# The low parts of the weights: 11/16 of each half on VectorE, 5/16 on GpSimd

## The chip, the cores and the metric

The kernel runs on one core of one Trainium2 chip. The metric is the device time of one execution in microseconds, as the median of three runs; less is better. The engines are TensorE (PE), VectorE (DVE), ScalarE (ACT), GpSimd (POOL) and the DMA queue of SyncE (SP).

## The reference

Two transformer-like blocks in float32 on 256 tokens of width 1024, batch 1. What matters here is only that nearly all of it is products of a small activation with large weights that are each used once:

```python
def first_block(x, ...):
    h = _rmsnorm(x, g_mix_pre)
    proj = h @ w_in + b_in                 # 1024 x 3328: pool, q, k, v, two gates
    y_pool = _multiscale_pool(...); y_attn = _sliding_window_sink_attention(...)
    merged = g_pool * (y_pool @ w_branch_pool) + g_attn * (y_attn @ w_branch_attn)
    x = x + _rmsnorm(merged @ w_out, g_mix_post)
    h2 = _rmsnorm(x, g_mlp_pre)
    return x + _rmsnorm(square(relu(h2 @ w_up)) @ w_down, g_mlp_post)   # hidden width 4096

def second_block(x, c, ctx, ...):          # two layers, latent and context rows
    for i in range(2):
        modulation = silu(c) @ mod_w[i] + mod_b[i]      # 1024 x 6144, shift, scale and gate
        o = short_conv_mixer(...) if i == 0 else mla_mixer(...)
        h = h + g1 * o
        h = h + g2 * swiglu(modulate(rms_norm(h), sh2, sc2), w_gate, w_up, w_down)  # hidden width 2816
    return h_lat
```

## The kernel before

To reach float32 accuracy, each product is made of three matmuls on split operands: a value is written as `hi + lo`, where `hi` is the value rounded to the type that TensorE reads (fp32r) and `lo` is the rest; the products are hi x hi, lo x hi and hi x lo (lines 401 to 403, in `product`). The modulation vectors need two (lines 435 and 436, in `mod_product`).

The weights come as one stream of 107 chunks, in the order of their use. A chunk is 128 partitions by 4096 columns (2 MB; some are 3072, 2304, 2048 or 1024 columns wide). Everything about it is double-buffered in two slots: `raw` (as loaded), `w_hi` and `w_lo`. For each chunk:

- SyncE's queue loads it into `raw` (line 328) as soon as `w_lo` of the chunk two before, which used the same slot, is complete (`lo_ready`).
- ScalarE waits for the load and for the products that read this slot last, and writes `w_hi` in two halves (line 947), each of which raises `hi_ready`.
- VectorE subtracts, `w_lo = raw - w_hi`, in two halves (line 1430, in `split`), each of which raises `lo_ready`.
- TensorE waits for the first half's `lo_ready` in `chunk()` and for the second half's in `split_half(0)`, in the middle of the first product of the chunk, or where its first column of the second half is.

The halves are given by

```python
half = width // 2
return [(h * half, (h + 1) * half) for h in range(2)]
```

The engines run their programs strictly in order. Where a split stands between the other work of ScalarE and VectorE is written out by hand. VectorE has much other work: it takes products out of PSUM (`gated<-bank,gate`, line 1792; `h<-silu,bank`, line 1843), adds to the residual rows (`x<-x,gated`, line 1794), makes the low parts of the activations (`act_lo`, line 1455; `h_lo`, lines 1707, 1848 and 2058), applies the norms (`scaled`, lines 1468 and 1471; `post_norm`, lines 1529 and 1530). GpSimd has no program at all.

The stages in order of time: the first block's input projection, attention and branches to about 170 us; norms and modulation to 205; the MLP in 4 turns of 57 us to 434, each of six chunks, two of which are modulation chunks; norms to 475; the convolution mixer to 640; norms; the FFN of the first layer to 1030, its main part in 4 turns of 72 us with one modulation chunk each; latent attention with four groups of heads to 1290; the output projection and norm to 1335; the second FFN to the end.

Of the kernel before, what the change touches and what calls it, by code (L numbers as in the profile page):

```python
# [21 lines left out]
CHUNK = 4096  # L22
# [15 lines left out]
MH = 16  # L38
GH = 4
# [8 lines left out]
SECTIONS = (  # L48
    ("w_in", 2, 4096), ("w_kv", 1, 2048), ("w_gates", 4, 4096), ("w_branch", 4, 4096), ("w_out", 2, 4096), ("mod_scale", 2, 4096),
    ("mlp", 24, 4096), ("mod_gate0", 2, 4096), ("conv_in", 8, 3072), ("conv_out", 2, 4096),  # L50
    ("mod_gate1", 2, 4096), ("ffn0_first", 1, 4096), ("ffn0_half", 1, 2048), ("ffn0", 19, 4096),
    ("mod_gate2", 2, 4096), ("mla_in", 2, 4096), ("mod_gate3", 1, 4096), ("mla_q", 4, 2304), ("mla_kv", 4, 1024),
    ("mod_gate3_half", 1, 4096), ("mla_out", 2, 4096),
    ("ffn1", 16, 4096), ("ffn1_half", 1, 2048),
)
STREAM = sum(n for _, n, _ in SECTIONS)
# [60 lines left out]
def build(nc, a, out):  # L117
    f32, f32r = mybir.dt.float32, mybir.dt.float32r
    ACT, ALU, AX = mybir.ActivationFunctionType, mybir.AluOpType, mybir.AxisListType
# [4 lines left out]
    def at(name, shape, offset, dtype=f32):  # L124
        return nc.alloc_sbuf_tensor_at(name, shape, dtype, offset=base + offset)

    K = 1024
    raw = at("raw", [P, 2, CHUNK], 0)
    w_hi = at("w_hi", [P, 2, CHUNK], 32 * K, f32r)
    w_lo = at("w_lo", [P, 2, CHUNK], 64 * K, f32r)  # L130
# [99 lines left out]
    def table(name, n, parts=P, j=0):  # L230
        return tab[0:parts, TAB[name] + j:TAB[name] + j + n]
# [15 lines left out]
    S = nc.alloc_semaphore  # L247
    loaded = [S("loaded0"), S("loaded1")]
    hi_ready = S("hi_ready")
    lo_ready = S("lo_ready")  # L250
    const_loaded = S("const_loaded")
    x_loaded = [S("x_loaded0"), S("x_loaded1")]
    bias_loaded = S("bias_loaded")
# [53 lines left out]
    WQ, WKV = QKT * GH * QK, KVT * COLS  # L307

    def halves_of(width):


        half = width // 2
        return [(h * half, (h + 1) * half) for h in range(2)]

    with nc.Block() as block:


        @block.sync
        def _(sp):
            n = Count()  # L320

            def load(section, k, width):
                c = n.step("chunk")
                slot = (n.n["chunk"] - 1) % 2
                if n.n["chunk"] > 2:
                    sp.wait_ge(lo_ready, 2 * n.at("chunk", 2))
                src = a[section][k] if isinstance(k, int) else a[section][bass.ds(k, 1)].rearrange("o p n -> (o p) n")
                sp.dma_start(raw[:, slot, 0:width], src).then_inc(loaded[slot], 16)


            for t in range(NT):
                sp.dma_start(x[:, t, :], a["x"][t * P:(t + 1) * P, :]).then_inc(x_loaded[t], 16)
            sp.dma_start(tab[:, :], a["tab"]).then_inc(const_loaded, 16)
            sp.dma_start(cols[:, :], a["cols"]).then_inc(const_loaded, 16)
            sp.dma_start(rows[:, :], a["rows"].rearrange("(o n) -> o n", o=1).to_broadcast([P, NROW])).then_inc(const_loaded, 16)
            for section, chunks, width in SECTIONS:
                first = 0
                if section == "mla_kv":
                    continue
                if section == "mla_q":  # L340
                    with n.loop(sp, chunks, chunk=2) as i:
                        load("mla_q", i, WQ)
                        load("mla_kv", i, WKV)
                    continue
                while first < chunks and (chunks < 8 or n.n["chunk"] < 2):
                    load(section, first, width)
                    first += 1
                turns = (chunks - first) // 2
                if turns:
                    with n.loop(sp, turns, chunk=2) as i:  # L350
                        load(section, i * 2 + first, width)
                        load(section, i * 2 + first + 1, width)
                if (chunks - first) % 2:
                    load(section, chunks - 1, width)

            for t in range(NT):
                sp.wait_ge(x_ready, X_UPDATES - NT + 1 + t)
                sp.dma_start(out[t * P:(t + 1) * P, :], x[:, t, :]).then_inc(out_done, 16)
            sp.wait_ge(out_done, 16 * NT)


        @block.tensor
        def _(te):
            n = Count()

            def chunk():
                n.step("chunk")
                split_half(1)
                return (n.n["chunk"] - 1) % 2

            def split_half(back):

                te.wait_ge(lo_ready, 2 * n.at("chunk") - back)

            def weights(s, j0, j1):
                return w_hi[:, s, j0:j1], w_lo[:, s, j0:j1]
# [14 lines left out]
            def product(dst, terms, second=None, also=None, before_last=None):  # L391


                for j, ((sh, sl), (mh, ml)) in enumerate(terms):
                    if before_last and j == len(terms) - 1:
                        before_last()
                    if j == second:
                        split_half(0)
                        if also:
                            also()  # L400
                    te.matmul(dst, sh, mh, start=(j == 0), stop=False)  # L401
                    te.matmul(dst, sh, ml, start=False, stop=False)  # L402
                    last = te.matmul(dst, sl, mh, start=False, stop=(j == len(terms) - 1))  # L403
                return last
# [21 lines left out]
            def mod_product():  # L426
                s = chunk()
                m = n.step("mod")
                if n.n["mod"] > 1:
                    te.wait_ge(mod_row_ready, n.at("mod", 1))  # L430
                for k in range(KT):
                    if k == KT // 2:
                        split_half(0)
                    h, l = weights(s, k * COLS, (k + 1) * COLS)
                    te.matmul(mod_ps[:, :], cond_w[:, k, :], h, start=(k == 0), stop=False)  # L435
                    last = te.matmul(mod_ps[:, :], cond_w[:, k, :], l, start=False, stop=(k == KT - 1))  # L436
                last.then_inc(mod_done, 1)
# [30 lines left out]
            for k, width in enumerate((COLS, COLS, 256)):  # L468
                s = chunk()
# [184 lines left out]
            s = chunk()  # L654
# [45 lines left out]
            s = chunk()  # L700
            for tt in range(2 * NT):
                conv_out(s, tt, tt == 0)
            s = chunk()
# [55 lines left out]
            s = chunk()  # L759
# [7 lines left out]
            s = chunk()  # L767
# [7 lines left out]
            s = chunk()  # L775
            for tt in range(2 * NT):
# [3 lines left out]
                first = 0 if tt < NT else 256  # L780
# [147 lines left out]
        def _(act):  # L928
            n = Count()

            def split(width=CHUNK):
                n.step("split")
                c = n.n["split"]
                if c > STREAM:
                    return
                s = (c - 1) % 2
                turns = 16 * ((c + 1) // 2)
                if n.turn is not None:
                    turns = n.turn * (8 * n.per["split"]) + turns
                act.wait_ge(loaded[s], turns)  # L940
                if n.n["unit"]:
                    act.wait_ge(gemm_done, n.at("unit"))
                if n.n["mod"]:
                    act.wait_ge(mod_done, n.at("mod"))
                for first, end in halves_of(width):
                    part = slice(first, end)
                    act.activation(w_hi[:, s, part], raw[:, s, part], ACT.Copy).then_inc(hi_ready, 1)  # L947

# [72 lines left out]
            for k in range(3):  # L1021
                split()
                n.step("unit", 2)
# [390 lines left out]
        def _(ve):  # L1414
            n = Count()
# [6 lines left out]
            def split(width=CHUNK):  # L1422
                n.step("split")
                if n.n["split"] > STREAM:
                    return
                s = (n.n["split"] - 1) % 2
                for half, (first, end) in enumerate(halves_of(width)):
                    part = slice(first, end)
                    ve.wait_ge(hi_ready, 2 * n.at("split") - 1 + half)
                    ve.tensor_tensor(w_lo[:, s, part], raw[:, s, part], w_hi[:, s, part].bitcast(f32),  # L1430
                                     ALU.subtract).then_inc(lo_ready, 1)
# [126 lines left out]
            for t in range(NT):  # L1558
                heads = proj[:, t, Q0:V0].rearrange("p (h d) -> p h d", d=HD)
                lo, hi = heads[:, :, 0:8], heads[:, :, 8:16]  # L1560
                c = table("cos1", 8, j=8 * t).rearrange("p (o d) -> p o d", o=1).to_broadcast([P, 10, 8])
                s = table("sin1", 8, j=8 * t).rearrange("p (o d) -> p o d", o=1).to_broadcast([P, 10, 8])
# [650 lines left out]
```

## Time and profile before

| what | value |
|---|---|
| time, median of 3 runs | 1531.93 us (1528.47 to 1532.8) |
| the profiled execution: its time, its span | 1531.93 us, 1530.1 us |
| TensorE busy, matmuls | 1435.3 us, 94% of the span |
| VectorE busy | 923.9 us, 60% |
| of that, the subtractions for `w_lo` (214) | 460.3 us |
| ScalarE busy | 651.2 us, 43% |
| GpSimd busy | 0.2 us, 4 instructions |
| mean granted clock of TensorE | 0.969 of full speed |
| loaded from memory | 213.7 MB, 140 GB/s |

The profile is of one execution. Busy time is the time in which an engine executes an instruction; waits on semaphores are not in it. Matmuls overlap one another, so that one lasts longer than the distance to the next. In the rows below an arrow in brackets names what ended the idle time in front of an instruction.

### The profile page before, as it was taken

To read this page: it belongs to the slowest core of one execution; us is meant where nothing else is said; L and a number is where in the kernel's file an instruction comes from. 1 tells how busy PE (TensorE), PEld (TensorE's weight loads), DVE (VectorE), ACT (ScalarE), POOL (GpSimd) and SP (SyncE) were. 2 spreads that over 40 slices of the span, in tenths; PEclk is the share of its full clock that TensorE was granted. 3 is DMA by queue.
4 is the path that set the end of the run, shared out by engine and by line. 5 is a ranking of instruction groups with operands and counts; after the bars stand their busy time and mean duration, and the time that the engine had idled before them with its cause. 6 is when DMAs were issued, how large, how long until landed. Compare 5 with 4: busy or idle time off the path is not lost.

```text
span 1530.1 us, 18989 instructions
## 1 busy us (share of the span) xinstructions
PE 1435.3 (94%) x7536; PEld 1208.1 (79%) x7536; DVE 923.9 (60%) x1136; ACT 651.2 (43%) x743; POOL 0.2 (0%) x4
## 2 busy tenths in 40 slices
PE   6999889999989999999999999998989988899998
PEld 5877678888867887777888888886867766699997
DVE  5677676765666655766444453537566656646567
ACT  5364555544552222543132322225535554543442
POOL 0000000000000000000000000000000000000000
PEclk9999989999999999999999999999879998899999
DMA  8525565655642233233332414213221121344541
GB/s 307 196 94 219 196 234 217 229 208 222 245 154 83 83 143 118 75 118 127 148 120 99 163 56 164 96 69 121 93 76 46 69 96 61 120 166 171 203 175 56
DMA packets 18152, 215.58 MB, mean 141 GB/s; under 512 B 1960, under 2 KB 2984, under 8 KB 4784
## 3 DMA queue, kind: packets, MB, share of 16 engines
q1 hardware_dynamic: 16416, 209.67, 36.6%
q10 hardware_dynamic: 1680, 5.13, 0.9%
q8 instruction: 40, 0.66, 0.2%
q14 instruction: 16, 0.13, 0.0%
HBM read 213.74 MB, written 1.05 MB: 140 GB/s over the span
## 4 chain that ended last, share of the span: by engine, by line
PE 81%; DVE 10%; ACT 5%; issue 2%; ACTq 0%; DMA 0%; DVEq 0%
PE bank L401 24%; PE bank L403 23%; PE bank L402 23%; DVE w_lo L1430 6%; PE turned L418 3%; ACT w_hi L947 3%; PE small L831 2%; PE bank L825 2%; PE mod_ps L435 1%; PE mod_ps L436 1%; PE small L448 1%; PE small L458 1%; DVE x L1794 0%; DVE gated L1792 0%; DVE scaled L1471 0%
## 5 line engine op out<-in xcount | busy, mean ns | idle before, releaser
L1430 DVE TENSOR_TENSOR w_lo<-raw,w_hi 128x2048 fp32r<-128x2048 f32 (+1 forms) x214 | 460.3, 2193 | 82.5 <-ACT w_hi L947 82.1
L947 ACT ACTIVATE w_hi<-raw 128x2048 fp32r<-128x2048 f32 (+1 forms) x214 | 380.7, 1827 | 247.4 <-PE bank L403 179.9
L401 PE MATMUL bank<-act_hi,w_hi 128*128 128x256 f32 (+1 forms) x1208 | 400.1, 331 | 21.2 <-DVE w_lo L1430 12.8
L402 PE MATMUL bank<-act_lo,w_hi 128*128 128x256 f32 (+1 forms) x1208 | 396.7, 328 | 0.0
L403 PE MATMUL bank<-act_hi,w_lo 128*128 128x256 f32 (+1 forms) x1208 | 396.6, 328 | 0.0
L401 PEld LDWEIGHTS bank<-act_hi,w_hi 128*128 128x128 f32 x1208 | 232.4, 192 | 52.8 <-issue 17.8
L402 PEld LDWEIGHTS bank<-act_lo,w_hi 128*128 128x128 f32 x1208 | 232.5, 192 | 19.4
L403 PEld LDWEIGHTS bank<-act_hi,w_lo 128*128 128x128 f32 x1208 | 232.4, 192 | 19.2
L401 PE MATMUL bank<-w_hi,h_hi 128*128 128x512 f32 x392 | 157.3, 401 | 2.7 <-DVE h_lo L1848 1.5
L402 PE MATMUL bank<-w_lo,h_hi 128*128 128x512 f32 x392 | 155.9, 398 | 0.0
L403 PE MATMUL bank<-w_hi,h_lo 128*128 128x512 f32 x392 | 155.8, 397 | 0.0
L1843 DVE TENSOR_TENSOR h<-silu,bank 128x512 f32<-128x512 f32 x22 | 15.1, 687 | 133.7 <-PE bank L403 133.7
L401 PEld LDWEIGHTS bank<-w_hi,h_hi 128*128 128x128 f32 x392 | 74.4, 190 | 21.1 <-DVE h_lo L1848 2.5
L401 PE MATMUL bank<-w_hi,act_hi 128*128 128x512 f32 (+1 forms) x224 | 85.8, 383 | 4.9 <-DVE w_lo L1430 3.6
L403 PEld LDWEIGHTS bank<-w_hi,h_lo 128*128 128x128 f32 x392 | 74.3, 189 | 17.8
L435 PE MATMUL mod_ps<-w_hi,cond_w 128*128 128x512 f32 x192 | 79.9, 416 | 8.7 <-DVE w_lo L1430 5.1
L402 PEld LDWEIGHTS bank<-w_lo,h_hi 128*128 128x128 f32 x392 | 74.3, 189 | 16.8
L402 PE MATMUL bank<-w_lo,act_hi 128*128 128x512 f32 (+1 forms) x224 | 84.7, 378 | 0.0
L403 PE MATMUL bank<-w_hi,act_lo 128*128 128x512 f32 (+1 forms) x224 | 84.6, 378 | 0.0
L1792 DVE TENSOR_TENSOR gated<-bank,gate 128x512 f32<-128x512 f32 x84 | 57.7, 687 | 41.1 <-PE bank L403 40.8
L436 PE MATMUL mod_ps<-w_lo,cond_w 128*128 128x512 f32 x192 | 78.3, 408 | 0.0
L1246 ACT ACTIVATE h_hi<-h 128x512 fp32r<-128x512 f32 x22 | 13.8, 628 | 97.2 <-DVE h L1843 97.2
(235 smaller groups left out, 1604.0 us busy)
## 6 DMA issues: line engine op xcount, KB each, us to landing
raw<-in_ffn SPq DMA_DIRECT2D x35, 2048.0 KB, 7.6
raw<-in_mlp SPq DMA_DIRECT2D x24, 2048.0 KB, 8.4
raw<-in_mod_gate SPq DMA_DIRECT2D x7, 2048.0 KB, 8.2
raw<-in_conv_in SPq DMA_DIRECT2D x8, 1536.0 KB, 6.5
raw<-in_w_gates SPq DMA_DIRECT2D x4, 2048.0 KB, 8.4
raw<-in_w_branch SPq DMA_DIRECT2D x4, 2048.0 KB, 8.6
raw<-in_mla_q SPq DMA_DIRECT2D x4, 1152.0 KB, 5.1
raw<-in_w_in SPq DMA_DIRECT2D x2, 2048.0 KB, 13.1
```

The costliest lines, as they stand in the source:

```text
L401: te.matmul(dst, sh, mh, start=(j == 0), stop=False)
L402: te.matmul(dst, sh, ml, start=False, stop=False)
L403: last = te.matmul(dst, sl, mh, start=False, stop=(j == len(terms) - 1))
L418: last = te.transpose(dst[0:m, j * P:(j + 1) * P], src, ident)
L435: te.matmul(mod_ps[:, :], cond_w[:, k, :], h, start=(k == 0), stop=False)
L436: last = te.matmul(mod_ps[:, :], cond_w[:, k, :], l, start=False, stop=(k == KT - 1))
L448: last = te.matmul(small[:, 2 * j:2 * j + 2], mod_row[0:4, j * P:(j + 1) * P], table("sel_col", 2, 4), start=True, stop=True)
L825: te.matmul(bank[u % 2][:, :], qgT[:, h, t * P:(t + 1) * P], kgT[:, h, :], start=True, stop=True).then_inc(scores_done, 1)
L831: last = te.matmul(small[:, u * VD:(u + 1) * VD], prT[:, u % 2, j, :], vg[:, j, h, :], start=(j == 0), stop=(j == 3))
L947: act.activation(w_hi[:, s, part], raw[:, s, part], ACT.Copy).then_inc(hi_ready, 1)
L1430: ve.tensor_tensor(w_lo[:, s, part], raw[:, s, part], w_hi[:, s, part].bitcast(f32), ALU.subtract).then_inc(lo_ready, 1)
L1792: ve.tensor_tensor(gated[:, k, :], b[:, :], gate[:, g, cb * COLS:(cb + 1) * COLS], ALU.mult).then_inc(gemm_read, 1)
```

## The change

The subtraction of each half is divided between two engines. Of a half's columns VectorE keeps the first 11/16 and GpSimd, which gets a program of its own, takes the last 5/16. GpSimd waits for the same `hi_ready` values as VectorE and raises a semaphore of its own, `lo_ready_pool`; the load queue and TensorE wait for both. ScalarE's conversion still goes by whole halves. The number and the order of the other instructions stay as they are.

```diff
+    lo_ready_pool = S("lo_ready_pool")
...
-        return [(h * half, (h + 1) * half) for h in range(2)]
+        return [(h * half, h * half + half * 11 // 16, (h + 1) * half) for h in range(2)]
...
                     sp.wait_ge(lo_ready, 2 * n.at("chunk", 2))
+                    sp.wait_ge(lo_ready_pool, 2 * n.at("chunk", 2))
...
+        @block.gpsimd
+        def _(pool):
+            n = Count()
+
+            def split(width=CHUNK):
+                n.step("chunk")
+                s = (n.n["chunk"] - 1) % 2
+                for _, share, end in halves_of(width):
+                    part = slice(share, end)
+                    pool.wait_ge(hi_ready, n.step("half"))
+                    pool.tensor_tensor(w_lo[:, s, part], raw[:, s, part], w_hi[:, s, part].bitcast(f32),
+                                       ALU.subtract).then_inc(lo_ready_pool, 1)
+
+            def splits(chunks):
+                with n.loop(pool, chunks // 2, chunk=2, half=4):
+                    split()
+                    split()
+                if chunks % 2:
+                    split()
+
+            names = [name for name, _, _ in SECTIONS]
+            before = sum(c for _, c, _ in SECTIONS[:names.index("mla_q")])
+            groups = MH // GH
+            splits(before)
+            with n.loop(pool, groups, chunk=2, half=4):
+                split(WQ)
+                split(WKV)
+            splits(STREAM - before - 2 * groups)
...
                 te.wait_ge(lo_ready, 2 * n.at("chunk") - back)
+                te.wait_ge(lo_ready_pool, 2 * n.at("chunk") - back)
...
-                for first, end in halves_of(width):
+                for first, _, end in halves_of(width):
                     part = slice(first, end)
                     act.activation(w_hi[:, s, part], raw[:, s, part], ACT.Copy).then_inc(hi_ready, 1)
...
-                for half, (first, end) in enumerate(halves_of(width)):
-                    part = slice(first, end)
+                for half, (first, share, _) in enumerate(halves_of(width)):
+                    part = slice(first, share)
                     ve.wait_ge(hi_ready, 2 * n.at("split") - 1 + half)
                     ve.tensor_tensor(w_lo[:, s, part], raw[:, s, part], w_hi[:, s, part].bitcast(f32),
                                      ALU.subtract).then_inc(lo_ready, 1)
```

GpSimd's program goes by chunks of 4096 columns throughout except in the attention section; the widths of the narrower sections outside it (`w_kv`, `conv_in`, `ffn0_half`, `ffn1_half`) are taken as 4096 there, as they are in VectorE's and ScalarE's programs, which convert the whole slot.

## Rows read from the trace of the kernel before

**Rows 1.** The page: the span, busy time, and shares of the chain that ended last.

```profile
span 1530.1 us, 18989 instructions
...
PE 1435.3 (94%) x7536; PEld 1208.1 (79%) x7536; DVE 923.9 (60%) x1136; ACT 651.2 (43%) x743; POOL 0.2 (0%) x4
...
PE 81%; DVE 10%; ACT 5%; issue 2%; ACTq 0%; DMA 0%; DVEq 0%
PE bank L401 24%; PE bank L403 23%; PE bank L402 23%; DVE w_lo L1430 6%; PE turned L418 3%; ACT w_hi L947 3%; PE small L831 2%; PE bank L825 2%; PE mod_ps L435 1%; PE mod_ps L436 1%; PE small L448 1%; PE small L458 1%; DVE x L1794 0%; DVE gated L1792 0%; DVE scaled L1471 0%
```

**Rows 2.** Groups by line and form on VectorE: busy us, mean ns | idle before.

```profile
L1430 DVE TENSOR_TENSOR w_lo<-raw,w_hi 128x2048 fp32r<-128x2048 f32 x198 | 444.6, 2288 | 81.8 <-ACT w_hi L947 81.5 <-DVE z_pad L1756 0.3
...
L1471 DVE TENSOR_SCALAR scaled<-turned,coef,mod_col 128x128 f32<-128x128 f32 x112 | 37.1, 403 | 12.0 <-PE turned L418 11.8
...
L1430 DVE TENSOR_TENSOR w_lo<-raw,w_hi 128x1152 fp32r<-128x1152 f32 x8 | 10.5, 1355 | 0.6 <-ACT w_hi L947 0.6
```

**Rows 3.** The chain that ended last, in an MLP turn: start us, us, what.

```profile
274.53 1.93 ACT w_hi L947
```

**Rows 4.** Who waited for whom on TensorE: us in total, times, longest us.

```profile
PE bank L401 <- DVE w_lo L1430: 18.5, 18, 3.6
PE mod_ps L435 <- DVE w_lo L1430: 5.1, 2, 3.2
```

**Rows 5.** Timeline of TensorE, waits for `w_lo`: start us, us, what [idle before].

```profile
18.59 0.80 PE L401 MATMUL bank<-w_hi,act_hi 128*128 128x512 f32 x1 [3.61 <-DVE w_lo L1430]
...
194.00 0.80 PE L435 MATMUL mod_ps<-w_hi,cond_w 128*128 128x512 f32 x1 [3.20 <-DVE w_lo L1430]
...
202.19 0.39 PE L401 MATMUL bank<-act_hi,w_hi 128*128 128x256 f32 x1 [1.48 <-DVE w_lo L1430]
...
204.39 0.38 PE L401 MATMUL bank<-act_hi,w_hi 128*128 128x256 f32 x1 [0.51 <-DVE w_lo L1430]
...
278.90 0.38 PE L401 MATMUL bank<-act_hi,w_hi 128*128 128x256 f32 x1 [0.69 <-DVE w_lo L1430]
...
281.03 0.39 PE L401 MATMUL bank<-act_hi,w_hi 128*128 128x256 f32 x1 [0.43 <-DVE w_lo L1430]
...
446.48 0.55 PE L401 MATMUL bank<-act_hi,w_hi 128*128 128x256 f32 x1 [3.01 <-DVE w_lo L1430]
...
721.46 0.49 PE L401 MATMUL bank<-act_hi,w_hi 128*128 128x512 f32 x1 [0.69 <-DVE w_lo L1430]
```

**Rows 6.** Timeline of TensorE inside a product of 512 columns.

```profile
260.08 0.39 PE L402 MATMUL bank<-w_lo,h_hi 128*128 128x512 f32 x1
260.31 0.40 PE L403 MATMUL bank<-w_hi,h_lo 128*128 128x512 f32 x1
```

**Rows 7.** Timeline of VectorE around splits (x2: two halves).

```profile
293.35 4.49 DVE L1430 TENSOR_TENSOR w_lo<-raw,w_hi 128x2048 fp32r<-128x2048 f32 x2 [1.25 <-ACT w_hi L947]
...
297.76 0.69 DVE L1707 TENSOR_TENSOR h_lo<-h,h_hi 128x512 fp32r<-128x512 f32 x1
...
436.80 4.49 DVE L1430 TENSOR_TENSOR w_lo<-raw,w_hi 128x2048 fp32r<-128x2048 f32 x2
...
719.03 4.49 DVE L1430 TENSOR_TENSOR w_lo<-raw,w_hi 128x2048 fp32r<-128x2048 f32 x2 [1.11 <-ACT w_hi L947]
...
1314.95 4.49 DVE L1430 TENSOR_TENSOR w_lo<-raw,w_hi 128x2048 fp32r<-128x2048 f32 x2 [0.58 <-ACT w_hi L947]
...
1320.08 0.69 DVE L1794 TENSOR_TENSOR x<-x,gated 128x512 f32<-128x512 f32 x1
...
1511.96 4.49 DVE L1430 TENSOR_TENSOR w_lo<-raw,w_hi 128x2048 fp32r<-128x2048 f32 x2 [1.39 <-ACT w_hi L947]
```

**Rows 8.** Waits of the load queue: us in total, times, longest us.

```profile
SPq L328 <- DVE w_lo L1430: 1425.1, 105, 37.0
```

**Rows 9.** Stretches: us, busy us of each engine (count), granted clock, DMA share, GB/s.

```profile
185.00:200.00 15.00, 9.16 (x32) 7.28 (x31) 10.34 (x14) 10.45 (x12) 0.00 (x0) 0.55 0.47 164
...
720.00:1030.00 310.00, 307.13 (x1348) 250.24 (x1347) 144.34 (x140) 86.01 (x76) 0.00 (x0) 1.00 0.30 115
```

## The prediction

> **What bounds the kernel now.** I read five views in this order. The busy shares and the chain of waits come first: TensorE is busy 94% of the span, VectorE 60%, GpSimd not at all, and the chain that ended last lies 81% on TensorE and 10% on VectorE, 6% of it on the one line that the change touches, the subtraction that makes `w_lo` [rows 1]. So the kernel is bound by matmuls, and a faster or slower split counts only where TensorE stands and waits for it. The grouped lines give the durations [rows 2, 3]. The waits of TensorE say how much there is: 18 waits of 18.5 us and 2 of 5.1 us, 23.6 us in all, for `w_lo` [rows 4]. The timelines say where and why [rows 5 to 8]. Last, the clock: in the stretch around the longest waits the granted clock is 0.55 of full speed, that is, mostly the lower of its two levels (1.2 against 2.4 GHz), and in the long FFN loop it is 1.00 [rows 9].
>
> Why TensorE waits: a chunk can be converted only when the chunk that last used its slot is consumed. From then ScalarE needs 1.93 us for the first half [rows 3], VectorE 2.29 us more [rows 2]. The chunk that TensorE works on meanwhile covers this, unless it is a modulation chunk: 16 matmuls at a pitch of 0.23 us [rows 6], 3.7 us. 1.93 + 2.29 = 4.2 us is longer; the wait of 0.69 us at 278.90 is about this difference, and the 0.43 us at 281.03 is the second half coming late as well [rows 5]. The two halves of a chunk, back to back on VectorE, take 4.49 us [rows 7].
>
> **What the change does, part by part.** Of each half of 2048 columns VectorE keeps 1408 and GpSimd takes 640; of the query chunks' halves of 1152 columns 792 and 360, of the key-value chunks' halves of 512 columns 352 and 160. All waiters now wait for both semaphores.
> VectorE's share: the rows of 2048 and 1152 columns (2288 and 1355 ns) give 1.041 ns for a column and 155 ns fixed [rows 2]. So 1408 columns take 155 + 1466 = 1.62 us, 0.67 us less than now; over 198 halves that alone frees 132 us of VectorE, nearly all of it beside other work.
> GpSimd's share: the trace has nothing but four tiny memsets on that engine. Bounds for 640 columns from the nearest rows: VectorE's own rate gives 155 + 666 = 0.82 us; the slowest per column of the larger VectorE groups, 403 ns for 128 columns [rows 2], or 3.15 ns a column, gives 2.0 us. It is between ends far apart and I take the middle, 1.4 us. The Trainium skill, GPSIMD Engine Reference, section Performance versus the Vector engine, gives a two-input operation on GpSimd 1.96 times VectorE's time; by it this would be 1.6 us and the loss below about a quarter larger. No run here shows it yet.
> The waits: the load queue waits for `w_lo` 105 times, 1425 us together [rows 8]; it is idle most of the time and waits one semaphore more, which is late only if GpSimd is. Nothing stands behind this wait but the next load. TensorE's extra wait instruction has nothing of its own; I cost both at nothing as long as GpSimd's share is not last. If it is, raw comes free later by the same amount, and where ScalarE already waits for the weights that is paid there.
>
> **The step that decides.** Both engines are released by the same semaphore and read the same two tensors, `raw` and `w_hi`, in the same microsecond. Either the two shares run side by side, and a half is ready after the longer one, 1.62 us; or they take turns, and it is ready after 1.62 + 1.41 = 3.03 us instead of 2.29. Even at the lower bound, 1.62 + 0.82 = 2.44 us, turns lose, because the fixed cost is paid twice. No row of before has the two engines at work together, so this is a choice. I take turns as the likelier, at 7 in 10: a subtraction reads two tensors for each column, twice the reading of a copy, and an engine that works beside it at full rate would have to find as much again.
> The Trainium skill, SBUF — State Buffer, section Who interferes with whom, says that a VectorE instruction with two SBUF inputs and a GpSimd instruction that reads SBUF exclude each other, and the later one stands for the whole of the other. By it a half takes 3.03 us and the change loses; without it 1.62 us and it gains. This speaks against the change more than anything else, and it would also hold back every other two-input VectorE instruction that meets a GpSimd share. No trace so far shows it.
>
> **The sum with turns.** The first half is ready 0.73 us later. The second: VectorE's part can begin only when GpSimd's first is over, at 3.03 us, so the pair takes 6.06 us for 4.49: 1.55 us later. By place:
> - first chunk, first half (18.59 [rows 5]): +0.7.
> - 194 to 204: the modulation chunk's half and the chunk after it, both halves exposed (3.20, 1.48, 0.51 [rows 5]); the first shift is mostly taken up by VectorE's own share being done only 0.16 us later: +0.2, then +1.55. Together 1.8.
> - the first modulation chunk of each of the 4 MLP turns (0.69 and 0.43 [rows 5]): 4 x 1.55 = 6.2.
> - the second modulation chunk of these turns. Now its successor is just in time: halves ready at 295.6 and 297.8, then `h_lo` at 297.76, which the down projection needs before its second half [rows 7]. `h_lo` has two SBUF inputs and would stand behind GpSimd until 299.4; it is done at 300.1, and the products of the first half (12 at 0.23 us from about 296.4) end at 299.2: +0.95 x 4 = 3.8.
> - 436.80: here VectorE itself is the chain: two halves, then the post-norm of two SBUF inputs, then the next half, for which TensorE waits 3.01 us [rows 5, 7]: 1.55 + 0.73 = 2.3.
> - the 4 turns of the first FFN (0.69 at 721.46 [rows 5]): the first half +0.73; the second was ready 0.76 us ahead of need (719.03 + 4.49 [rows 7] against 721.46 + 12 x 0.235), so 1.55 - 0.76 = 0.8 decides: 3.2.
> - where VectorE's residual addition `x<-x,gated` (two SBUF inputs) follows a split on the chain: 1320.08 would wait until 1314.95 + 6.06 = 1321.0, +0.9 [rows 7]; the split at 1511.96 [rows 7] in front of the last additions the same; two more places alike (about 690 and 1035): 3.4.
> - the other waits of [rows 4] and the small halves of the four attention groups: an estimate from the same differences, 3.5.
> Together 0.7 + 1.8 + 6.2 + 3.8 + 2.3 + 3.2 + 3.4 + 3.5 = 24.9 us. The rest of the 107 splits lies under matmuls of 11 us and more and costs nothing; if that cover were gone, each chunk would cost 1.5 us, 160 us in all. The profiled execution took 1531.93 us (span 1530.1 and 1.8 around it), which is also the median of the three runs. 1531.9 + 24.9 = about 1557 us.
> With GpSimd's bounds: 0.82 us makes the pair 4.88 us, +0.39 for +1.55, a quarter of the sum, +6: 1538. 2.0 us makes it 7.24 us, 1.8 times the sum, +45: 1577.
>
> **The rivals.**
> Side by side (faster). If the shares do not disturb one another and GpSimd's is under 2.29 us, the first half comes 0.67 us sooner and the second, which ScalarE's 1.93 us then sets, 0.94 us sooner. The waits of [rows 5] give: first chunk 0.67, 194 to 204 0.67 + 0.94, MLP turns 4 x 0.94, the post-norm place 2 x 0.67 + 0.67, FFN turns 4 x 0.67, two others about 1; 12 us. Where VectorE stands before the chain's next step (471, 1290, 1315, 1512) about 1 us each, 4 to 5. Together -17: 1515 us; with GpSimd at its 2.0 us a half gains 0.29 us, -8: 1524. For it: VectorE's time does fall. Against it: nothing in the trace says that both can read at once. It decides from the point at which the two shares together take less than 2.29 us.
> No change. The two engines disturb each other partly, and a half takes as long as before: 1532. It needs a coincidence, a half of 2.2 to 2.4 us.
> The other mishap, a GpSimd share so slow that side by side does not help (over 2.29 us for 640 columns, 3.3 ns a column), lies beyond the slowest row that I have; it would land inside the first case's range.
> The clock. Longer waits in the stretches that are already at 0.55 lengthen them; a doubled pitch over some 5 us of matmuls costs 2 to 3 us. That is inside the range. The FFN loop stayed at 1.00 with its short waits.
>
> **How the numbers follow.** Turns 0.70, side by side 0.22, no change 0.08. What a measurement of this kernel can tell from no change is about 0.3%, 4.6 us; the lower end of the first case, +6, is above it. Its own range is 1538 to 1577. To hold 8 in 10 the range must reach down into the faster case: 1513 to 1577. The predicted time is that of the first case, 1557.
>
> **What would show it.** With turns: VectorE's `w_lo` of 1408 columns reads longer than 1.62 us, or starts late after its release, or GpSimd's row of 640 columns ends 3 us after the release; start to start of two halves is near 3 us; `h_lo` or `x<-x,gated` behind a split stands about 0.9 us; TensorE's wait near 279 is about 1.4 us and near 281 about 1.3 us, now for GpSimd's line. Side by side: 1.62 us on VectorE, both waits gone or near 0.2 us, ScalarE's conversion last in the chain. I am wrong in kind if the shares overlap in full at unchanged durations; in size if GpSimd is far from 1.4 us, or if waits appear in chunks that I took as covered.

## The result and the profile after

The changed kernel takes 1554.61 us (median of 4 runs, 1550.21 to 1558.37), the kernel before 1530.26 us in the same comparison (1528.47 to 1532.8): a ratio of 1.0156, 95% interval 1.0134 to 1.0179. It is slower by 24.4 us; the forecast was 1557 us, by the shares taking turns. The profiled execution has a span of 1551.2 us, 21.1 us over the one before. It is the fastest of the seven executions on record of the changed kernel; the other six took 1552.67 to 1558.37 us.

The page of the changed kernel, beside [rows 1]: span, busy time, shares of the chain that ended last.

```profile
span 1551.2 us, 19862 instructions
...
PE 1434.6 (92%) x7536; PEld 1202.8 (78%) x7536; DVE 975.3 (63%) x1136; ACT 651.0 (42%) x743; POOL 551.3 (36%) x218
...
issue 44%; PE 29%; POOL 19%; DVE 5%; ACT 3%; POOLq 0%; ACTq 0%; DVEq 0%
```

VectorE gave away 31% of each subtraction and is busy 51 us longer. GpSimd went from nothing to 551 us, and it is now on the chain. The groups by form on VectorE and GpSimd, beside [rows 2], say where that comes from (busy us, mean ns | idle before).

```profile
L1463 DVE TENSOR_TENSOR w_lo<-raw,w_hi 128x1408 fp32r<-128x1408 f32 x198 | 454.4, 2309 | 94.7 <-ACT w_hi L980 94.5 <-DVE z_pad L1789 0.3
L1825 DVE TENSOR_TENSOR gated<-bank,gate 128x512 f32<-128x512 f32 x84 | 57.5, 684 | 35.8 <-PE bank L436 35.6
L1827 DVE TENSOR_TENSOR x<-x,gated 128x512 f32<-128x512 f32 x56 | 46.6, 832 | 1.9
...
L1740 DVE TENSOR_TENSOR h_lo<-h,h_hi 128x512 fp32r<-128x512 f32 x16 | 21.9, 1370 | 10.9 <-ACT h_hi L1172 10.9
...
L374 POOL TENSOR_TENSOR w_lo<-raw,w_hi 128x640 fp32r<-128x640 f32 x198 | 536.5, 2727 | 869.7 <-ACT w_hi L980 868.9
```

1408 columns last 2309 ns on average, longer than 2048 columns did before (2288 ns), though their own work is 1.62 us. `h_lo` went from 0.69 us [rows 7] to 1.37 us and `x<-x,gated` from 0.69 us [rows 7] to 0.83 us; both read two tensors in SBUF, the memory that also holds `raw`, `w_hi` and `w_lo`. `gated<-bank,gate` has the same shape but reads one of its two inputs from PSUM, where the products lie. It still takes 0.684 us, and so do the 13 of its 84 records that overlap one of GpSimd's (0.68 us). So the lengthening does not belong to VectorE as such, but to its instructions with two SBUF inputs.

The timeline of VectorE, then that of GpSimd, at one MLP turn's first modulation chunk (start us, us, what [idle before]), the place of the chain row [rows 3].

```profile
285.00 1.63 DVE L1463 TENSOR_TENSOR w_lo<-raw,w_hi 128x1408 fp32r<-128x1408 f32 x1 [0.80 <-ACT w_hi L980]
286.80 2.71 DVE L1463 TENSOR_TENSOR w_lo<-raw,w_hi 128x1408 fp32r<-128x1408 f32 x1 [0.18 <-ACT w_hi L980]
289.43 2.02 DVE L1740 TENSOR_TENSOR h_lo<-h,h_hi 128x512 fp32r<-128x512 f32 x1
...
285.05 5.87 POOL L374 TENSOR_TENSOR w_lo<-raw,w_hi 128x640 fp32r<-128x640 f32 x2 [2.67 <-ACT w_hi L980]
```

Read it as four turns. VectorE's first share runs undisturbed for 1.63 us while GpSimd's, recorded as begun, stands. Then GpSimd works, and VectorE's second share, recorded from 286.80, takes 2.71 us for 1.62 us of work: it stood 1.09 us. Then `h_lo` stands 1.33 us behind GpSimd's second share. The pair is complete at 290.92, 5.92 us after the first release, where both halves took 4.49 us before [rows 7]. A GpSimd turn is (5.92 - 2 x 1.62) / 2 = 1.34 us.

TensorE's waits for the same places: totals by whom it waits for (us in total, times, longest), beside [rows 4],

```profile
PE bank L434 <- POOL w_lo L374: 27.4, 20, 4.4
...
PE bank L434 <- issue: 9.2, 6, 2.3
...
PE mod_ps L468 <- DVE w_lo L1463: 4.5, 2, 4.0
...
PE mod_ps L468 <- issue: 4.0, 1, 4.0
```

and its timeline, beside [rows 5].

```profile
19.29 0.77 PE L434 MATMUL bank<-w_hi,act_hi 128*128 128x512 f32 x1 [4.38 <-POOL w_lo L374]
...
136.84 0.47 PE L434 MATMUL bank<-w_hi,yattn_hi 128*128 128x512 f32 x1 [2.08 <-POOL w_lo L374]
...
158.03 0.47 PE L434 MATMUL bank<-w_hi,act_hi 128*128 128x512 f32 x1 [2.03 <-POOL w_lo L374]
...
288.26 0.38 PE L434 MATMUL bank<-act_hi,w_hi 128*128 128x256 f32 x1 [1.53 <-POOL w_lo L374]
...
291.06 0.36 PE L434 MATMUL bank<-act_hi,w_hi 128*128 128x256 f32 x1 [1.11 <-POOL w_lo L374]
...
743.28 0.49 PE L434 MATMUL bank<-act_hi,w_hi 128*128 128x512 f32 x1 [1.52 <-POOL w_lo L374]
```

The 23.6 us of [rows 4] became 27.4 + 4.5 us under a name, and 13.2 us are put down to "issue", a releaser that the profile does not see (2.3 us of it before); its 4.0 us stand where the 3.20 us of [rows 5] stood. The load queue, which waited 1425 us for VectorE [rows 8], now waits 1356 us for GpSimd, and in 35 of the 105 cases 88 us more for VectorE. By the ends of the second shares GpSimd is last in 71 of the 107 chunks and VectorE in 36. The waits of 0.69 and 0.43 us at 278.90 and 281.03 [rows 5] are 1.53 and 1.11 us at 288.26 and 291.06.

Where the 21.1 us lie, from the same instruction in both traces (the two traces' start times, their difference): end of the MLP, the last `mlp<-bank,mlp`, 433.54 and 449.91, +16.4; the first `x<-x,gated` after the long FFN loop, 1034.75 and 1060.83, +26.1; the second one after latent attention, 1313.68 and 1333.11, +19.4; end, +21.1. (The first one after latent attention stands on VectorE behind two shares in the changed kernel, and its +20.9 is not yet what TensorE sees.) So 16.4 us are lost up to the end of the MLP and 9.7 us up to the end of the first FFN; 6.6 us are given back in attention, and 1.6 us are lost behind it. The give-back was not foreseen.

### The profile page after: what moved, and what is told of

It is laid out like the page before. It is cut to its first block, busy times and chain, and to the rows that moved or that the text cites. A ratio compares the mean times of both kernels' runs of the same rounds, so it can differ in the third digit from the quotient of the medians.

```text
span 1551.2 us, 19862 instructions
## 1 busy us (share of the span) xinstructions
PE 1434.6 (92%) x7536; PEld 1202.8 (78%) x7536; DVE 975.3 (63%) x1136; ACT 651.0 (42%) x743; POOL 551.3 (36%) x218
## 4 chain that ended last, share of the span: by engine, by line
issue 44%; PE 29%; POOL 19%; DVE 5%; ACT 3%; POOLq 0%; ACTq 0%; DVEq 0%
POOL w_lo L374 19%; PE bank L434 8%; PE bank L435 8%; PE bank L436 8%; PE turned L451 2%; PE bank L858 2%; PE small L864 1%; DVE w_lo L1463 1%; ACT w_hi L980 1%; DVE gated L1825 1%; DVE x L1827 1%; DVE scaled L1504 1%; PE mod_ps L468 0%; PE mod_ps L469 0%; DVE stat L1993 0%
## 5 line engine op out<-in xcount | busy, mean ns | idle before, releaser
L374 POOL TENSOR_TENSOR w_lo<-raw,w_hi 128x640 fp32r<-128x640 f32 (+1 forms) x214 | 551.1, 2591 | 986.7 <-ACT w_hi L980 985.7
L1463 DVE TENSOR_TENSOR w_lo<-raw,w_hi 128x1408 fp32r<-128x1408 f32 (+1 forms) x214 | 466.4, 2195 | 95.5 <-ACT w_hi L980 95.1
L434 PE MATMUL bank<-act_hi,w_hi 128*128 128x256 f32 (+1 forms) x1208 | 400.2, 331 | 28.7 <-POOL w_lo L374 17.3
L435 PEld LDWEIGHTS bank<-w_lo,h_hi 128*128 128x128 f32 x392 | 74.1, 189 | 16.4
```

Of the source, the lines that this page charges most:

```text
L374: pool.tensor_tensor(w_lo[:, s, part], raw[:, s, part], w_hi[:, s, part].bitcast(f32), ALU.subtract).then_inc(lo_ready_pool, 1)
```

## The experiments

The first four kernels ran on one chip beside the kernel before (1530.20 us, 15 runs), the last three on another (1531.62 us, 17 runs).

**One SBUF input on VectorE.** From the third chunk on, VectorE's share is a reduction over the same 1408 columns of `raw` alone, into one column of `w_lo`; these low parts are then not computed. Everything else is the changed kernel. It takes away the second SBUF input, and no wait.

```diff
-                    ve.tensor_tensor(w_lo[:, s, part], raw[:, s, part], w_hi[:, s, part].bitcast(f32),
-                                     ALU.subtract).then_inc(lo_ready, 1)
+                    if n.turn is None and n.n["split"] <= 2:
+                        ve.tensor_tensor(w_lo[:, s, part], raw[:, s, part], w_hi[:, s, part].bitcast(f32),
+                                         ALU.subtract).then_inc(lo_ready, 1)
+                    else:
+                        ve.tensor_reduce(w_lo[:, s, first:first + 1], raw[:, s, part], AX.X, ALU.max).then_inc(lo_ready, 1)
```

> From the third chunk on VectorE's share is no subtraction of two tensors but a maximum over the same 1408 columns of raw alone (its low parts keep old values, so the result of the kernel is not the reference's). GpSimd's share, the waits and all else stay as in the changed kernel. My theory, turns between two instructions that both need a second SBUF read path: a maximum of 1408 columns reads one tensor and lasts about 1.6 us as well, GpSimd's 640 columns run beside it in 1.4 to 1.55 us (its one undisturbed row of the changed kernel is 1.54), a pair ends about 3.6 us after the release instead of 5.9, and the kernel takes 1513 to 1520 us. Rival A, any VectorE instruction that reads SBUF excludes GpSimd: rows of about 3 us on GpSimd as now and 1555 us. Rival B, GpSimd is just slow to start or slow beside a busy chip, whoever works on VectorE: also about 3 us on GpSimd and 1555 us.

Measured: 1504.81 us, ratio 0.9837 (0.9819 to 0.9855). The timeline of VectorE and GpSimd at the same MLP turn:

```profile
276.94 1.62 DVE L1467 TENSOR_REDUCE w_lo<-raw 128x1 fp32r<-128x1408 f32 x1 [1.66 <-ACT w_hi L980]
...
276.98 1.58 POOL L374 TENSOR_TENSOR w_lo<-raw,w_hi 128x640 fp32r<-128x640 f32 x1 [2.31 <-ACT w_hi L980]
```

and the two groups of the whole execution:

```profile
L1467 DVE TENSOR_REDUCE w_lo<-raw 128x1 fp32r<-128x1408 f32 x194 | 313.0, 1619 | 108.9 <-ACT w_hi L980 108.4 <-DVE z_pad L1792 0.2
...
L374 POOL TENSOR_TENSOR w_lo<-raw,w_hi 128x640 fp32r<-128x640 f32 x198 | 320.5, 1619 | 1031.5 <-ACT w_hi L980 1031.2
```

Both start together and end together. GpSimd's 640 columns fall from 2.73 us on average to 1.62 us, and nothing of GpSimd's own was changed. (The usual record is the 1.58 us shown above; the mean of 1619 ns holds the four halves of the first two chunks, which VectorE still subtracts and which last about 3 us, and a few that meet other two-input instructions. Four of GpSimd's halves meet no work of VectorE's, and they last 1.57 to 1.58 us too.) With GpSimd at 1.6 us and no exclusion, the kernel is faster than before; 50 us lie between this and the changed kernel. The reduction differs from the subtraction in one more way, it writes only one column; its 1.62 us are just what the subtraction of 1408 columns was worked out to take. That the missing writes make the difference is ruled out by `gated<-bank,gate` of the changed kernel, which writes 512 columns into SBUF beside GpSimd and loses nothing. The Trainium skill, SBUF — State Buffer, section Who interferes with whom, says just this: an instruction of VectorE with two SBUF inputs and one of GpSimd that reads SBUF exclude each other. By that rule, the traces agree, on both sides of it (2.31 and 2.73 us with two inputs, 1.62 and 1.62 us with one).

It came out below what was expected. The same landmarks as above say where: 8.3 us gained up to the end of the MLP, 9.0 us up to the end of the FFN, and 10.2 us in attention. My sum for shares side by side had priced no gain of that size in attention.

**Sixteen columns on GpSimd.** The changed kernel with the smallest share; it keeps every wait and every GpSimd instruction.

```diff
-        return [(h * half, h * half + half * 11 // 16, (h + 1) * half) for h in range(2)]
+        return [(h * half, h * half + half - 16, (h + 1) * half) for h in range(2)]
```

> GpSimd takes only the last 16 columns of each half, VectorE the rest. Turns: a half takes VectorE's 2.27 us plus GpSimd's fixed part, 0.2 to 0.25 us, so 2.5 us for 2.29; the loss of 0.78 us a half cost 24 us, so this costs 6 to 8 us: 1536 to 1539 us. If the loss came from the columns given to GpSimd alone, and the extra waits and the second participant were free: 1530 us.

Measured: 1530.30 us, 0.9997 (0.9985 to 1.0008): missed, no loss at all. VectorE and GpSimd at an MLP turn:

```profile
278.89 4.48 DVE L1463 TENSOR_TENSOR w_lo<-raw,w_hi 128x2032 fp32r<-128x2032 f32 x2 [0.86 <-ACT w_hi L980]
...
278.93 4.51 POOL L374 TENSOR_TENSOR w_lo<-raw,w_hi 128x16 fp32r<-128x16 f32 x2 [4.08 <-ACT w_hi L980]
```

The pair takes 4.5 us, as without GpSimd. GpSimd's record of a 16-column half lasts as long as VectorE's half; nearly all of it is standing, for 13 of these halves meet no work of VectorE's and last 0.22 us each. So its fixed part is spent while it waits for its turn and costs nothing. Two things follow: the added semaphore, its waits on TensorE and on the load queue and 214 more instructions cost nothing that the times show, as the prediction had it (by stages, in the table below, it is +2.8 us up to the end of the MLP and -4.0 us behind it); and "the fixed cost is paid twice", as the prediction also had it, is wrong.

**256 columns on GpSimd**, the same edit with `half - 256`.

> GpSimd takes the last 256 columns of each half. Turns: GpSimd's rows of 640 and 160 columns undisturbed (1.54 and 0.54 us) give 2.08 ns a column and 0.21 fixed, so 256 columns take 0.74 us after VectorE's 2.02: 2.76 us for a half, 0.47 later than before, 0.6 of the changed kernel's loss: 1543 to 1547 us. Side by side with mutual slowing would give less than 2.2 us for the half and a time at or below 1530 us.

Measured: 1535.22 us, 1.0039 (1.0026 to 1.0051): the right sign, but too high an expectation.

```profile
280.19 4.50 DVE L1463 TENSOR_TENSOR w_lo<-raw,w_hi 128x1792 fp32r<-128x1792 f32 x2 [0.84 <-ACT w_hi L980]
284.61 1.21 DVE L1740 TENSOR_TENSOR h_lo<-h,h_hi 128x512 fp32r<-128x512 f32 x1
...
280.24 5.03 POOL L374 TENSOR_TENSOR w_lo<-raw,w_hi 128x256 fp32r<-128x256 f32 x2 [3.54 <-ACT w_hi L980]
```

VectorE's own work for 1792 columns is 0.155 + 1.041 x 1.792 = 2.02 us, so a GpSimd turn is (5.03 - 2 x 2.02) / 2 = 0.50 us, 1.9 ns a column; with 640 columns it is 1.34 us, 2.1 ns a column; with 16 it is about nothing. The law of the turn has a slope of about 2 ns and hardly a constant. A column moved costs 2.1 and saves 1.04, so each moved column of a half costs about 1.06 ns: 0.68 us for 640. Of the changed kernel's 24.4 us, 256 columns would be worth 0.27 / 0.68, 9.7 us; measured were 5.0 us. The stages in the table below point to where the other 4.7 us are: up to the end of the MLP the loss is in proportion (6.4 us, 16.4 x 0.27 / 0.68 = 6.5), but the FFN loses 1.0 us where 3.9 would be in proportion, and attention gives back 6.1 us of the 6.6, although the share is much smaller.

**Quarters instead of halves, GpSimd idle.** In the kernel before, ScalarE and VectorE go by quarters, and VectorE raises `lo_ready` after the second and the fourth. This shortens the latency that the change was up against, 1.93 us of ScalarE and then 2.29 us of VectorE, with no second engine.

```diff
-                for first, end in halves_of(width):
+                for first, end in quarters_of(width):
...
-                    ve.wait_ge(hi_ready, 2 * n.at("split") - 1 + half)
-                    ve.tensor_tensor(w_lo[:, s, part], raw[:, s, part], w_hi[:, s, part].bitcast(f32),
-                                     ALU.subtract).then_inc(lo_ready, 1)
+                    ve.wait_ge(hi_ready, 4 * n.at("split") - 3 + quarter)
+                    low = ve.tensor_tensor(w_lo[:, s, part], raw[:, s, part], w_hi[:, s, part].bitcast(f32), ALU.subtract)
+                    if quarter % 2:
+                        low.then_inc(lo_ready, 1)
```

> The kernel before, GpSimd not used; ScalarE converts and VectorE subtracts in quarters of a chunk, the two low halves are announced as before. If what costs is that the first half is late at the exposed places: ScalarE's two quarters take about 1.96 us, the second quarter's subtraction 1.2 us, so the first half is ready after 3.2 us instead of 4.2 and the second after 5.6 instead of 6.4; 0.85 to 1.0 us at each of the exposed places, 12 to 17 us in all: 1514 to 1519 us. Rival: the additional instructions' fixed cost (about 0.15 us each on both engines, 214 more each) lies on the path as well and eats it: 1530 us or more.

Measured: 1515.25 us, 0.9894 (0.9871 to 0.9918), as expected. The waits of TensorE, beside [rows 4]:

```profile
PE bank L404 <- DVE w_lo L1433: 10.4, 9, 2.9
...
PE mod_ps L438 <- DVE w_lo L1433: 6.9, 3, 2.5
```

20 waits of 23.6 us became 12 of 17.3 us, though VectorE's group grew from 444.6 us [rows 2] to 458.1 us. The waits were made by latency in a few places, not by VectorE's load.

**GpSimd only in latent attention.** The kernel before, but with GpSimd taking 5/16 of the nine chunks of latent attention (four groups' query and key-value chunks and the chunk behind them) and of no other. The load queue's loop over these chunks is written out. It asks whether the 6.6 us that the changed kernel got back there are its own doing.

```diff
+    def shared(c):
+        return first_shared < c <= first_shared + 9
...
-                for half, (first, end) in enumerate(halves_of(width)):
-                    part = slice(first, end)
+                for half, (first, share, _) in enumerate(halves_of(width, shared(n.n["split"]))):
+                    part = slice(first, share)
```

> GpSimd takes its 5/16 only in the nine chunks of the latent attention section, where VectorE is busy with other work when the halves become ready and GpSimd's rows in the changed kernel last 1.5 us for 640 columns; everywhere else VectorE subtracts alone as before. Theory, turns: there GpSimd has read its columns before VectorE comes to its own, so each chunk costs VectorE 1.3 us less (halves of 2048) or 0.3 to 0.6 us less, on a chain in which VectorE matters: 2 to 4 us less in all, 1526 to 1528 us. If the loss were tied to the extra waits or to GpSimd's work as such, wherever it stands: 1531 us or more.

Measured: 1527.75 us, 0.9972 (0.9961 to 0.9984), as expected: 3.9 us less, where the whole change costs 24. VectorE and GpSimd around the last of these chunks:

```profile
1246.03 1.78 DVE L1980 TENSOR_TENSOR qg<-qg,rows 128x256 f32<-128x256 f32 x1
1250.67 3.15 DVE L1460 TENSOR_TENSOR w_lo<-raw,w_hi 128x1408 fp32r<-128x1408 f32 x2
1255.12 0.35 DVE L1952 TENSOR_TENSOR qr_t<-qg,tab 128x64 f32<-128x64 f32 x2
...
1245.88 3.33 POOL L380 TENSOR_TENSOR w_lo<-raw,w_hi 128x640 fp32r<-128x640 f32 x2 [17.72 <-ACT w_hi L977]
```

The same place on VectorE in the kernel before:

```profile
1248.15 0.42 DVE L1950 TENSOR_TENSOR qg<-qg,rows 128x256 f32<-128x256 f32 x1
...
1252.79 4.48 DVE L1430 TENSOR_TENSOR w_lo<-raw,w_hi 128x2048 fp32r<-128x2048 f32 x2
1258.58 0.35 DVE L1922 TENSOR_TENSOR qr_t<-qg,tab 128x64 f32<-128x64 f32 x2
```

Here the split is written behind other work of VectorE. GpSimd has its share done at 1249.21, before VectorE comes to its own at 1250.67, which then runs undisturbed: 3.15 us for 4.48 us. The next step, `qr_t`, was 2.12 us early plus this 1.33 us: 3.46 us early at 1255.12. The price is one standing in front, `qg` of 256 columns in 1.78 us for 0.42 us, behind which VectorE is idle until 1249.06 anyway. Whoever comes first has the turn; what matters is who is late next. How much of the 3.9 us goes this way is looked at behind the table.

**Eighths.** As the quarters, with eight pieces.

> As the quarters, with eight pieces of 512 columns. A piece costs ScalarE 0.55 to 0.6 us and VectorE 0.61 us (pitch of its rows of 512 columns), so VectorE becomes the slower of the two: first half after 3.0 to 3.1 us, second after 5.5, hardly earlier than with quarters (3.2 and 5.6), and a split whose pieces are all ready costs 4.9 instead of 4.6 us. 1513 to 1518 us, the same as quarters; clearly below that only if finer pieces keep paying, above 1520 us if the fixed cost decides.

Measured: 1516.39 us, 0.9901 (0.9887 to 0.9916), no better than quarters. VectorE's group:

```profile
L1433 DVE TENSOR_TENSOR w_lo<-raw,w_hi 128x512 fp32r<-128x512 f32 x792 | 485.0, 686 | 9.7 <-ACT w_hi L950 8.1 <-DVE z_pad L1760 0.3
```

485.0 us for 458.1 with quarters and 444.6 with halves [rows 2]: each cut buys less latency, and each further instruction adds 0.07 us to VectorE (26.9 us for 396 more).

**Quarters, and GpSimd in latent attention.** The last two put together, GpSimd's share cut from the second and the fourth quarter of these nine chunks.

> Quarters everywhere and GpSimd's 5/16 of each half in the attention section alone. If the two gains are independent, the quarters' 15 us and the 2 to 4 us of the attention section add: 1511 to 1513 us. If they are the same gain seen twice, 1515 us.

Measured: 1512.51 us, 0.9877 (0.9863 to 0.9892), the fastest version here, 19 us under the kernel before. Its interval overlaps that of the quarters alone, on another chip, so that GpSimd's part adds to the quarters is not shown by the times. The stages speak for it only in part. The gain (-) or loss (+) of each profiled execution against that of before, in us, by the three landmarks named above and the span:

| kernel | to the end of the MLP | to the end of the FFN | attention | rest |
|---|---|---|---|---|
| the change | +16.4 | +9.7 | -6.6 | +1.6 |
| one SBUF input | -8.3 | -9.0 | -10.2 | -0.2 |
| 16 columns | +2.8 | -3.3 | -0.7 | 0.0 |
| 256 columns | +6.4 | +1.0 | -6.1 | -0.2 |
| quarters | -8.3 | -6.3 | -0.1 | -0.3 |
| GpSimd in attention only | -0.5 | -0.3 | -3.6 | 0.0 |
| eighths | -8.5 | -5.1 | -3.0 | -0.3 |
| quarters and GpSimd there | -8.2 | -3.9 | -7.2 | -1.3 |

A stage can move by some us without a change in its own split: in attention the eighths gain 3.0 us with no GpSimd at all. Much of a difference in attention is the granted clock. Windows over the same 1262 matmuls (us, busy us of each engine, granted clock, DMA share, GB/s), before, after, and with GpSimd in attention only:

```profile
1041.07:1313.60 272.53, 246.36 (x1262) 199.85 (x1263) 172.12 (x328) 141.05 (x246) 0.00 (x0) 0.90 0.21 77
```

```profile
1067.14:1333.04 265.90, 238.37 (x1262) 192.03 (x1263) 177.39 (x328) 140.80 (x246) 47.67 (x30) 0.93 0.21 77
```

```profile
1040.27:1309.23 268.96, 243.46 (x1262) 197.42 (x1263) 172.34 (x328) 141.01 (x246) 17.73 (x18) 0.91 0.21 78
```

In the changed kernel TensorE is busy 8.0 us less for the same matmuls, at 0.93 for 0.90, and its idle time grows from 26.2 to 27.5 us. So the 6.6 us given back are matmul time at a higher clock and not shorter waits. With GpSimd in attention only, 2.9 of the 3.6 us are busy time and 0.7 us idle time. What raised the clock stays open: the earlier VectorE may have done it, or the state in which the kernel enters attention; no run held the one fixed.

## Why the prediction was right, and where it was off

**Turns or side by side.** Right: turns. The signs named ahead were all there: 1408 columns read longer than 1.62 us; `h_lo` and `x<-x,gated` stand; waits of "about 1.4 and 1.3" near 279 and 281 were 1.53 and 1.11 us, and named GpSimd's line. That the second SBUF input does it, and not the reading of GpSimd as such, is shown by the kernel with one SBUF input, and by `gated<-bank,gate`, which also writes as much as `h_lo` and does not stand.

**GpSimd's duration.** Undisturbed it takes 1.58 us for 640 columns, in a turn 1.34; the forecast took 1.4 us for both. The pair is 5.92 us for the 6.06 forecast, near because the sum had added a fixed part that is hidden under the standing. The Trainium skill, GPSIMD Engine Reference, section Performance versus the Vector engine, gives the factor 1.96, by which the estimate was 1.6 us; the trace agrees for GpSimd undisturbed (1.58 us), not for the turn that decides here.

**"Even at the lower bound turns lose, because the fixed cost is paid twice."** Wrong, as 16 columns showed. Turns lose because a column costs 2.1 ns on one engine and 1.04 ns on the other, and by that slope no share pays where both are released together.

**"That alone frees 132 us of VectorE."** Not in the records: 51 us more, since an instruction that stands for its turn counts as busy.

**The terms.** First chunk +0.7, forecast 0.7 (19.29 against 18.59 [rows 5]). The stretch from 194 to 205 us +1.7, forecast 1.8. MLP turns: +2.6 us each with 59.45 us for 56.84, forecast 2.5; over the whole MLP 10.6 us, forecast 10.0. FFN turns +0.92 us each, 3.7 in all, forecast 3.2. These carry the sum, and their mechanism is as written.
The branches of the first block were taken as covered and were not. TensorE waits 2.08 us at 136.84 and 2.03 us at 158.03 for GpSimd's share, and at the second of them it is 2.5 us late, not 0.7. In the kernel before, these places read

```profile
135.25 0.47 PE L401 MATMUL bank<-w_hi,yattn_hi 128*128 128x512 f32 x1 [1.19 <-issue]
...
155.57 0.47 PE L401 MATMUL bank<-w_hi,act_hi 128*128 128x512 f32 x1 [1.14 <-issue]
```

so both were waits already, under a name that the list for `w_lo` [rows 4] does not hold. Behind the second, matmuls follow at 0.43 us for 0.23 (granted clock 0.72 from 158.0 to 164.2, and 1.00 from 155.5 to 160.0 before), which adds 1.6 us. By the modulation chunks TensorE is 4.1 us late: +3.4 us, forecast nothing. Waits in chunks taken as covered were named ahead as a sign of being wrong in size.
The post-norm place after the MLP, forecast 2.3 us, cost 0.5 us net. At its matmul of 446.48 (465.83 after) TensorE is 3.0 us later than at the end of the MLP, but a wait for `c_sb` at 476.65 (493.42) is 1.84 us for 3.17, and the rest comes back between the two.
The last two terms, 3.4 and 3.5 us, stood for everything else: 6.9 us, with 0.5 us measured. The norms and the first chunk of the first FFN cost 4.1 us, 1.4 of it in a new wait for the normed rows `xn` and 2.1 in three waits for `w_lo`. At 1034.75 the addition is 1.4 us later than TensorE, because a small `coef<-mod_col,cols` stood behind the second share in front of it. Attention gave back 6.6 us. At 1320.08 and at the last additions `x<-x,gated` stands 0.65 us each, forecast 0.9, and from attention to the end 1.6 us are lost.
For attention the term had the wrong sign. It held that "every other two-input VectorE instruction that meets a GpSimd share" is held back, and priced only that. Where VectorE is occupied with other work when the release comes, GpSimd has the turn first and the share is taken off VectorE, as the 1.33 us of the last attention chunk show. But TensorE's idle time there did not fall, so the give-back itself is the clock, whose rise no run explains.

So 24.9 us forecast, with 21.1 us between the profiled executions and 24.4 us between the medians, is nearer than the working deserves, and in part luck. Against the forecast the branches were +3.4 us, the MLP +0.6, the FFN turns +0.5, the stretch at 194 us -0.1, the post-norm place -1.8 and the rest -6.4: 24.9 + 4.5 - 8.3 = 21.1 us. A part that was left out and a part that was priced with the wrong sign cancel in part.

## What to carry to other kernels

Before part of an instruction goes to an idle engine, look where its inputs lie: a subtraction of two SBUF tensors on VectorE and GpSimd's share of it take turns, so that the sum of both is paid, and the smaller the share the smaller the loss. Give GpSimd such work only where VectorE is busy with something else at the time of the release; here that gave 4 us at most, part of it by the clock. And where the waits are few and made by the latency of two engines in a row, cut the pieces finer before adding an engine: quarters gained 15 us here where the second engine lost 24.

## What the runs showed of the hardware

- An instruction that stands for its turn is recorded as begun and busy: 16 columns on GpSimd read 4.51 us for two. A long mean in the profile can be a wait without the name of one.
- The start-up of a GpSimd instruction lies under this standing: a turn takes 0.50 us for 256 columns and 1.34 us for 640, but undisturbed records are 0.73 and 1.58 us long, and 0.22 us for 16 columns.
- A reduction of VectorE with one SBUF input (1.62 us for 1408 columns) and products with one input in PSUM (0.68 us for 512 columns) run beside GpSimd without a loss to VectorE; GpSimd's 640 columns take 1.58 us beside them.
- When GpSimd comes first, VectorE's instruction stands, however small: 256 columns of `qg` take 1.78 us for 0.42 us.
- TensorE's clock can fall behind a longer wait, and need not: behind the 2.03 us at 158.03 the granted clock was 0.72 where it had been 1.00, and 1.6 us more were lost; behind the 2.08 us at 136.84 nothing more was.
